# Up projections by tokens with square turning, and the latent attention one step deeper

## The reference, cut to what matters

```python
def sqrelu_mlp(x, w_up, w_down):            # twice, D_FF = 8192
    h = jax.nn.relu(x @ w_up)
    return (h * h) @ w_down

def _conv_ffn(h, w_up, conv_w, conv_b, w_down):   # once, D_FF_2 = 5632
    a = h @ w_up                                  # 2 * 5632 wide
    a = lax.conv_general_dilated(a, ..., padding=[(2, 0)], ...) + conv_b   # along tokens, per feature
    gate, val = jnp.split(a, 2, axis=-1)
    return (jax.nn.silu(gate) * val) @ w_down

def _mla_group(...):        # 8 heads, 128 + 64 wide queries and keys
    q = _rmsnorm(c_q) @ w_uq;  kv = _rmsnorm(c_kv) @ w_ukv;  rope on q_pe, k_pe
    s = (q_nope @ k_nope.T + q_pe @ k_pe.T) * scale, causal
    o = softmax(s) @ v

def _s5_group(...):         # state space, then
    y = gelu(y);  return y * sigmoid(y @ w_glu + b_glu)
```

## Time and profile before

| | |
|---|---|
| median of three timed runs | 3221.11 us (3218.59 to 3222.48) |
| profiled execution | span 3218.5 us from the first to the last instruction; the page has no other time of this execution |
| PE busy | 3177.3 us, 99% of the span |
| PE weight loads busy | 2784.9 us, 87% |
| DVE busy | 2108.8 us, 66% |
| ACT busy | 1461.3 us, 45% |
| POOL busy | 417.4 us, 13% |
| chain that ended last | PE 95%, DVE 2%, ACT 1%, issue 1% |
| mean granted TensorE clock | 0.995 |
| DMA | 614 MB, 191 GB/s on average |

### The profile page before, as it was taken

How to read it: one execution, slowest core, us unless ns; L and a number is a source line. 1 busy time by engine, 2 the same in 40 slices (tenths; PEclk the granted TensorE clock), 3 DMA queues, 4 the chain that set the end, 5 groups by cost and what they waited for, 6 DMA issues and landing times.

```text
span 3218.5 us, 45058 instructions
## 1 busy us (share of the span) xinstructions
PE 3177.3 (99%) x17462; PEld 2784.9 (87%) x17462; DVE 2108.8 (66%) x1924; ACT 1461.3 (45%) x1374; POOL 417.4 (13%) x562
## 2 busy tenths in 40 slices
PE   9999999999999999999999999999889999999998
PEld 9988888888889999988888888879878888888887
DVE  6777666566665555667666666677756776677767
ACT  5454444444453433454443443455654544444443
POOL 2112443344351000000000000005120000000000
PEclk9999999999999999999999999999999999999999
DMA  8555555555545544446555555545335555555553
GB/s 307 183 200 213 207 204 204 203 199 207 208 174 186 199 159 178 164 166 264 193 192 187 194 187 191 194 148 210 139 124 192 211 195 187 191 189 188 195 184 117
DMA packets 119674, 614.21 MB, mean 191 GB/s; under 512 B 13472, under 2 KB 42272, under 8 KB 53152
## 3 DMA queue, kind: packets, MB, share of 16 engines
q1 hardware_dynamic: 97280, 598.77, 51.3%
q10 hardware_dynamic: 22304, 14.16, 1.4%
HBM read 600.30 MB, written 12.58 MB: 190 GB/s over the span
## 4 chain that ended last, share of the span: by engine, by line
PE 95%; DVE 2%; ACT 1%; issue 1%; ACTq 0%; DVEq 0%
PE ps L2229 29%; PE ps L2236 15%; PE ps L2378 12%; PE ps L2379 11%; PE ps L2380 11%; PE ps L2212 2%; PE ps L2214 2%; PE ps L2213 2%; PE ps L2547 1%; PE ps L2548 1%; PE ps L2549 1%; DVE wlo L1238 1%; PE ps L2267 1%; PE ps L2273 1%; ACT whi L619 1%
## 5 line engine op out<-in xcount | busy, mean ns | idle before, releaser
L619 ACT ACTIVATE whi<-raw 128x2048 fp32r<-128x2048 f32 (+2 forms) x564 | 1032.1, 1835 | 1496.7 <-PE ps L2236 842.8
L1238 DVE TENSOR_TENSOR wlo<-raw,whi 128x2048 fp32r<-128x2048 f32 (+2 forms) x564 | 1236.2, 2199 | 494.9 <-ACT whi L619 494.2
L2229 PE MATMUL ps<-x_pair,whi 128*128 128x512 f32 x4032 | 962.2, 391 | 0.0
L2229 PEld LDWEIGHTS ps<-x_pair,whi 128*128 128x128 f32 x4032 | 743.7, 188 | 145.8
L2236 PEld LDWEIGHTS ps<-x_pair,wlo 128*128 128x128 f32 x4032 | 517.0, 191 | 19.6
L2236 PE MATMUL ps<-x_pair,wlo 128*128 128x256 f32 x4032 | 523.0, 283 | 0.0
L2378 PE MATMUL ps<-whi,hid_hi 128*128 128x512 f32 x1280 | 500.1, 391 | 0.1
L2379 PE MATMUL ps<-wlo,hid_hi 128*128 128x512 f32 x1280 | 498.5, 389 | 0.0
L2380 PE MATMUL ps<-whi,hid_lo 128*128 128x512 f32 x1280 | 498.2, 389 | 0.0
L1276 DVE TENSOR_TENSOR resid<-resid,ps 128x1024 f32<-128x1024 f32 x165 | 201.5, 1221 | 187.3 <-PE ps L2380 184.7
L2380 PEld LDWEIGHTS ps<-whi,hid_lo 128*128 128x128 f32 x1280 | 240.3, 188 | 50.5
(11 more groups left out here) (407 smaller groups left out, 3497.4 us busy)
## 6 DMA issues: line engine op xcount, KB each, us to landing
raw<-weights SPq DMA_DIRECT2D x513, 1024.0 KB, 4.8
raw<-weights SPq DMA_DIRECT2D x32, 768.0 KB, 4.2
read_tab<-read_tables SPq DMA_DIRECT2D x2, 3072.0 KB, 10.3
raw<-weights SPq DMA_DIRECT2D x8, 640.0 KB, 6.3
drive_tables<-drive_out ACTq DMA_DIRECT2D x16, 256.0 KB, 2.2
read_tables<-c_wide ACTq DMA_DIRECT2D x32, 128.0 KB, 2.1
drive_tab<-drive_tables SPq DMA_DIRECT2D x4, 1024.0 KB, 8.8
x_in<-x_t SPq DMA_DIRECT2D x4, 512.0 KB, 8.8
```

The source lines that it names most:

```text
L619: act.activation(whi[:, s, 0:width], raw[:, s, 0:width], ACT.Copy).then_inc(hi_ready, 1)
L1238: dve.tensor_tensor(wlo[:, s, 0:width], raw[:, s, 0:width], whi[:, s, 0:width].bitcast(F32), ALU.subtract).then_inc(lo_ready, 1)
L2229: ins = pe.matmul(o, whi[:, s, c], x_pair[:, k].rearrange("p h t -> p (h t)"), start=k == 0, stop=False)
```

## The change

What it does, part by part:

- **Up quads by tokens.** `up_rows` replaces `wide_block` and `wide_second`: for each chunk and both token halves, 12 matmuls that move 512 columns of weights, as in a down quad. The weights are packed for this on the host. The result is in two PSUM banks, tokens on partitions: banks 0 and 1 for all up quads of an MLP but the second (2 and 3); in the gated layer gates in 0 and 1, values in 2 and 3. PE needs `wlo` of a chunk before its first matmul now.
- **Square turning.** DVE transposes each 128 x 512 bank in squares of 32 x 32 into `turns` (two instructions per quad), and ACT moves the squares to their places with 16 instructions of 32 partitions by 256 numbers each (`move_up`), which also take the relu. The four sums of a quad, the relu and the `staged` copies and PE transposes of the three layers go away.
- **Order of DVE.** The two transposes come before the last `lo1` of a down quad, then the additions. In the gated layer two additions now come before the value's convolution, one came before.
- **Latent attention.** PE's loop becomes turn(h), scores(h + 1), mix(h), k projection of h + 2, q projection of h + 3, both halves of a gate product; the mla chunks come one place earlier against the glu chunks in `MIXER`.
- **Gelu.** The second square and both low parts move from ACT and DVE to POOL; five of the copies of y move from ACT to DVE, behind a wait for ACT's.

```diff
+            def move_up(b, dst, turns, func):
+                act.wait_ge(up_turned, b * 2 + 2)
+                for i in range(4):
+                    for j in range(4):
+                        src = turns[32 * i:32 * i + 32].rearrange("p t (k q c) -> p q t k c", q=4, c=32)[:, j]
+                        to = dst[32 * j:32 * j + 32].rearrange("p k (t i c) -> p i t k c", t=2, c=32)[:, i]
+                        ins = act.activation(to, src, func)
+                ins.then_inc(up_moved, 1)
+                act.wait_ge(up_moved, b + 1)
...
                 def activate(g):
-                    act.wait_ge(tile_summed, g * 4 + (WIDE[name] + 4))
-                    act.activation(hid[:], hid[:], ACT.Relu).then_inc(block_free, 1)
-                    act.wait_ge(block_free, g + (b0 + 3))
+                    if not (isinstance(g, int) and g == 0):
+                        act.wait_ge(hidden_lo, g + h0)
+                    move_up(g + UP[name], hid, up_turns, ACT.Relu)
                     act.activation(hid[:], hid[:], ACT.Square).then_inc(hidden_ready, 1)
...
+            def turn_up(turns, b, q, bank, tt, free=None):
+                if free is not None:
+                    dve.wait_ge(up_moved, free)
+                if tt == 0:
+                    dve.wait_ge(up_made, b + 1)
+                else:
+                    wait_used(dve, q)
+                dve.transpose(turns[:, tt, :], ps[:, bank + tt, :]).then_inc(up_turned, 1)
+
+            def lo4_turn(q, turns, b, q_up, bank, free=None):
+                for s in range(3):
+                    lo1(q, s)
+                for tt in range(2):
+                    turn_up(turns, b, q_up, bank, tt, free)
+                lo1(q, 3)
...
+            def up_rows(q, bank, turned_=None):
+                if turned_ is not None:
+                    pe.wait_ge(up_turned, turned_)
+                for s in range(SLOTS):
+                    chunk(q, s)
+                    for tt in range(2):
+                        ins = rows_tile(ps[:, bank + tt, :], s, tt, range(4 * s, 4 * s + 4), xhi, xlo, s == 0, s == 3)
+                        if tt == 0 and s == 3:
+                            ins.then_inc(up_made, 1)
+                    ins.then_inc(chunk_used, 1)
...
 # ACT, gated layer
                 conv_first(g, 1)
+                hi1(q + 1, 0)
+                hi1(q + 1, 1)
                 if last:
                     ffn_split(g, True)
-                hi4(q + 1)
+                hi1(q + 1, 2)
+                hi1(q + 1, 3)
...
 # DVE, gated layer, groups after the first
+                lo1(q, 1)
+                lo1(q, 2)
+                for tt in range(2):
+                    turn_up(pair_turns[1], g * 2 + (u0 + 1), q_up, 2, tt, None if first else g * 2 + u0)
+                lo1(q, 3)
+                add_down(q, 0)
+                add_down(q, 1)
+                value()
+                lo1(q + 1, 0)
...
 # ACT, latent attention
+            copy_out(2)
+            exps(3)
+            hi_mixer(22, 23)
+            copy_kv(4)
+            copy_q(5)
+            hi_mixer(23, 24)
+            for h in range(3, N_HEADS - 1):
+                copy_turned_mla(h)
+                glu_gate(h - 3)
+                copy_out(h)
+                exps(h + 1)
+                if h < N_HEADS - 2:
+                    copy_kv(h + 2)
...
+                hi_mixer(2 * h + 18, 2 * h + 19)
+                if h < N_HEADS - 3:
+                    copy_q(h + 3)
+                hi_mixer(2 * h + 19, 2 * h + 20)
...
 # DVE, latent attention
+            for h in range(3, N_HEADS - 1):
+                gate_y(h - 3)
+                softmax_in(h + 1)
...
+                softmax_out(h + 1)
+                lo_mixer(2 * h + 18, 2 * h + 19)
+                if h < N_HEADS - 3:
+                    rope_head(h + 3)
+                lo_mixer(2 * h + 19, 2 * h + 20)
...
 # PE, latent attention
+            mla_scores(0)
+            project_k(1)
+            project_q(2)
+            for h in range(N_HEADS - 1):
+                mla_turn(h)
+                mla_scores(h + 1)
+                mla_mix(h)
                 if h < N_HEADS - 2:
-                    project_q(h + 2)
-                    mla_turn(h)
-                    fill(h, 0)
-                    mla_mix(h)
-                    fill(h, 1)
+                    project_k(h + 2)
+                if h < N_HEADS - 3:
+                    project_q(h + 3)
+                if 2 <= h <= 5:
+                    fill_glu(h - 2, 0)
+                    fill_glu(h - 2, 1)
+            out_fill("out_ssm", 0, 0)
+            out_fill("out_ssm", 0, 1)
+            mla_turn(N_HEADS - 1)
```

More of the change, by code:

```diff
@@ L45 @@
 SCAN_DVE = 12
+Y_ACT = 11
 WARM = 20
@@ L2019, in split @@
                     dve.tensor_tensor(lo[:], hid[:], hi[:].bitcast(F32), ALU.subtract).then_inc(hidden_lo, 1)
-                if last:
-                    value()
-                for s in range(SLOTS):
-                    if adds:
-                        add_down(q, s)
-                    else:
-                        sum_tile(gate_sum, q, s, s)
+                if not adds:
+                    value()
+                    lo4_turn(q + 1, pair_turns[0], g * 2 + (u0 + 2), q, 0, g * 2 + (u0 + 1))
+                    split(hid_hi, hid_lo)
+                    return
+                add_down(q, 0)
+                add_down(q, 1)
+                value()
+                lo1(q + 1, 0)
+                if last:
+                    split(end_hi, end_lo)
+                lo1(q + 1, 1)
+                for s in range(2, SLOTS):
+                    add_down(q, s)
                     lo1(q + 1, s)
-                    if s == 0:
-                        split(end_hi, end_lo) if last else value()
                 if not last:
                     split(hid_hi, hid_lo)
-            lo4_first("ffn2", up_sum[:, 0], q0)
+            lo4_first(q0, pair_turns[0], u0)
             group(0, q0 + 2, q0 + 1, False)
@@ L2245, in wide_tile @@
                 wide_low(q, s, ps[:, bank, :], range(DT)).then_inc(chunk_used, n_used)
-            def wide_block(q, summed_, tables=None):
-                for s in range(4):
-                    pe.wait_ge(tile_summed, summed_ + s)
-                    if tables is not None and s == 2:
-                        pe.wait_ge(job_copied, tables)
-                        pe.wait_ge(lags_copied, tables)
-                    wide_tile(q, s, s, 1)
             def rows_first(name, q, width, between):
@@ L2456, in turn_next @@
                     turn_x("mlp0", resid, 0)
-                pe.wait_ge(block_free, b0 + 2)
                 rows_first(first, q0, 512, turn_other)
-                wide_second(first, q0 + 1, w0)
+                up_rows(q0 + 1, 2)
                 if tables:
@@ L2967, in mlp @@
     def mlp(up, down):
-        u, d = columns(up).reshape(-1, 4, P, CW), rows(down).reshape(-1, 4, P, CW)
-        parts = [rows(up[:, 0:512])]
+        u, d = blocks(up).reshape(-1, 4, P, CW), rows(down).reshape(-1, 4, P, CW)
+        parts = [u[0]]
         for g in range(len(u) - 1):
@@ L2974, in ffn @@
     def ffn(up, down):
-        u, d = columns(up).reshape(2, -1, 4, P, CW), rows(down).reshape(-1, 4, P, CW)
+        u, d = blocks(up).reshape(2, -1, 4, P, CW), rows(down).reshape(-1, 4, P, CW)
         n = len(d)
-        parts = [rows(up[:, 0:512]), u[1, 0]]
+        parts = [u[0, 0], u[1, 0]]
         for g in range(n - 1):
```

265 lines of the change are left out of this document (114 added, 151 removed).

## The result

| | before | after |
|---|---|---|
| median of the timed runs | 3220.91 us (3218.59 to 3222.48) | 3194.81 us (3193.11 to 3197.30) |
| ratio to the kernel before | | 0.9921, 95% interval 0.9909 to 0.9933 |
| span of the profiled execution | 3218.5 us | 3192.7 us |
| DVE, ACT, POOL busy | 2108.8, 1461.3, 417.4 us | 2034.8, 1767.4, 446.2 us |

The change takes 26.1 us off; 32.6 were forecast (3188 us, range 3170 to 3208). I read the profile after by landmarks: instructions of TensorE that both kernels have, whose starts are compared.

What follows compares the result with a forecast made beforehand. The prediction took PE, 99% busy, as the only bound. From the 3218.5 us span it subtracted 27.6 for up quads and 5 for latent attention, giving 3185.9; with 2.6 for the median it said 3188 us, range 3170 to 3208.

Steps and rivals of the forecast that it cites:

- Up quads: 27.6 forecast: PE in the three layers: 48 up quads gain 0.49 us each and three second quads 1.35, together 27.6 us.
- The rival by which columns alone count: Up quads: matmul time follows columns moved, so layers gain 0.1 us per quad; 3207 us, chance 0.04.
- What hides the moves: Between up and down quads, ACT's 16 moves take 6.2 us and cost nothing up to about 7.6 us.
- The named chain: MLP down quad: ACT's high part, moves, square, next high part, then DVE's low part and addition of chunk 1; 15.0 us.
- the named waiter: PE in an MLP down quad waits for the addition of down chunk 1 before chunk 3, at 16.3 us.
- The last down quads of each layer see the same cover, so no loss there.: End of each layer: the moves stay hidden as in the loop, so the loss is none.
- Latent attention: 5 us forecast: Latent attention stage: a gain of 10 or 4 us, taken as 5; bounds a gain of 24 and a loss of 6.
- the early wait: PE idles 3.5 us before the q projection of head 2, which waits for DVE's `rope_head(1)`.
- the slow clock behind the three waits: Latent attention: half clock after the long idles may add 2 us to each of three phases, 2396.4 instead of 2390.4.
- The forecast's first two rivals: Latent attention: all its idle goes, 3171 us, chance 0.14; or its waits slow the clock and it loses, 3200 us, 0.18.
- the deep pipeline: Latent attention: chunks are ready in time and all idle goes, 20 to 24 us gained; 3171 us, chance 0.14.
- the large term: Up quads by tokens on PE in the three layers: a gain of 27.6 us.

Runs made afterwards that it cites:

- The kernels with cut moves: The changed kernel with 8, then all 16, of each up projection's moves cut into two halves of 32x128: 3196.91 us and 3210.39 us.
- the attention part alone: The kernel before with only the new order of the latent attention, up projections unchanged: 3219.82 us, ratio 0.9998.
- the other form: The changed kernel with the scaling of the row maxima as scalar_tensor_tensor against a tile of ones instead of tensor_scalar: 3193.91 us, ratio 0.9918.
- all moves cut: The changed kernel with all 16 moves of every up projection cut into two halves of 32x128: 3210.39 us, ratio 0.9969.
- the work moved: The changed kernel with the two low parts of the gelu on DVE instead of POOL: 3193.19 us, ratio 0.9917.
- with the chunks in time: The changed kernel with the weight chunks of heads 5, 6 and 7 split one step earlier on ACT and DVE: 3174.21 us, ratio 0.9857.

## Why the prediction was right, and where it was off

**Up quads: 27.6 forecast.** Right in kind and nearly in size. 28 quads of the MLPs at 0.49 us and two second quads at 1.35 make 16.4; the landmarks give 16.0. The gated layer's 21 quads make 11.2; the landmarks give 9.9 with an idle of 1.81 in it, so 11.7 for the quads. The rival by which columns alone count would have given 0.1 us per quad; it is refuted by the 22.28 us of an old up quad against 21.76 of a new one.

**What hides the moves.** The named chain and the named waiter were right. The moves took 6.80 us and not 6.2, the transposes 0.71 and not 0.69, and the cover was still there: 1.1 us beyond the 6.80, so 7.9 where I had 7.6. The kernels with cut moves measured it: no wait in the loop at 7.55, one in every group of the second MLP at 8.27.

**The step that failed: "The last down quads of each layer see the same cover, so no loss there."** They don't in the gated layer. In its last group DVE's list has the split of the hidden block and two low parts ahead of the third addition, which the last down quad waits for; in the loop nothing waits there. I had read the loop and not the last group. It measured 1.8 us of idle, and 1.7 more to the end with the slow matmuls that followed in this execution, 3.5 in all. In the second MLP the sentence was wrong too, though it cost nothing: the last down quad but one had no cover left, as the cut moves show.

**Latent attention: 5 us forecast, 0.5 to 1.6 measured.** The mechanism was right: the q projections of heads 5, 6 and 7 waited for `wlo`, 5.96, 4.75 and 4.76 us (4.0, 5.2 and 5.2 forecast), the early wait was 3.27 (3.5), the long idle at the output products went. From turn(2) to the row sums I had 74.8 us at full clock; it took 84.3, 9.5 more. The terms that were too small: the slow clock behind the three waits, 5.7 us (5.3 of them in the three projections, 14.0 instead of 8.7), which the forecast had at 6 and used nearly whole, when it took 5 us of gain between 10 and 4; the wait ahead of the q projection of head 5, in the phase of head 2, longer by 2.0; and 1.2 at the last turn, where DVE makes the low part of a gated pair inside the softmax. The other two waits were 0.9 us shorter than forecast together; the 1.5 us that are left are spread over the phases, and no run takes them apart.

The wait of head 5 was longer for two reasons. The forecast let `softmax_in(3)` start 1.6 us behind turn(2); it started 3.5 us behind it (turn(2) is at 2298.48), because DVE's list has the low part of the first gate chunk ahead of it, and that waited for ACT. And the scaling of the maxima in it took 1.08 us, held by GpSimd, instead of 0.17:

```profile
2299.74 2.29 DVE L1256 TENSOR_TENSOR wlo<-raw,whi 128x2048 fp32r<-128x2048 f32 x1 [0.99 <-ACT whi L620]
2301.95 0.55 DVE L1849 TENSOR_TENSOR m_prob_buf<-ps,const 128x384 f32<-128x384 f32 x1
...
2303.18 1.08 DVE L1854 TENSOR_SCALAR row_max<-row_max 128x2 f32<-128x2 f32 x1
```

Against these losses turn(2) came 8.0 us earlier in its stage instead of 6.8, and that was luck of the execution: the forecast had a slow stretch behind the early wait, and in the traces here it came in four of the eight with that wait (the attention part alone, the other form, all moves cut, the work moved) and not in the other four, the profiled execution of the change among them. The forecast's first two rivals were the two ends of one scale: with the chunks in time the stage is 21.3 us shorter than before, as the deep pipeline's 20 to 24 us had it.

**The sum** was off by 6.8 us by the spans (3192.7 against 3185.9). The landmarks put 3.4 of it on the attention (5 forecast, 1.6 there) and 3.5 on the end of the gated layer; the quads themselves came out at 27.7 instead of 27.6. The number lies in its range because the large term was right; inside the attention, the early gain made good a part of what the later phases lost.

## What to carry to other kernels

A pipeline that is made deeper on one engine is only as deep as the preparation on the others: when a consumer moves a step ahead, look up in which step the other queues, in their written order, make what it reads. Read the last iteration of a loop on its own, since its order has other waiters. And price a long idle on TensorE at its length plus a stretch at half clock: here 14 us less of waiting brought 20. In these traces every idle of 3.5 us and more had such a stretch behind it, idles of 1.8 to 3.3 us had it in some executions and not in others. So before a difference of 1 or 2 us between two traces is put down to an edit, compare the granted clock of both.

## What the runs showed of the hardware

- A VectorE operation on 128x2 took 2.24 us instead of 0.17 beside a GpSimd operation on 128x1024, in two forms, and ended with it; taking the GpSimd work away brought 0.17 back.
- ACT copies between groups of partitions cost 6.80 us for 16 of 32x256 and 8.27 us for 32 of 32x128, with rows of 414 and about 300 ns each. The 32 overlap in part (32 times 300 ns would be 9.6 us), the 16 do not, so the length of a set is read from its first start and last end, and not from the mean of a row times the count.
- The same idle of 1.8 us ahead of the last down quads was followed by matmuls of up to 0.63 us in one execution (PEclk 0.79 in the window) and of 0.40 us in another. The same idle of 3.27 us ahead of the q projection of head 2 was followed by 5 us at a granted clock of 1.00 in one and of 0.50 in another.
